# A hybrid decoder step on one core: a mask moved ahead of two key steps, and eight value pages requested later

## The reference, cut to what matters

```
z   = (q . k) / sqrt(64) + bias                    # stick-breaking attention, 8 heads
w_s = exp(log_sigmoid(z_s) + sum_{j>s} log_sigmoid(-z_j))
ya  = sum_s w_s v_s
yb  = rmsnorm(GLA(q, k, v, decay)) * silu(r)        # gated linear attention
h  += (sigmoid(g_a) * (ya @ U_a) + sigmoid(g_b) * (yb @ U_b)) @ W_o
h  += sum over 8 x 16 chosen experts of gate * gelu(h_n . u_e) * v_e
h  += (p @ W_ple) * sigmoid(rmsnorm(h) @ W_gate)
```

## Time and profile before

| | |
|---|---|
| median of 3 runs | 2042.43 us (2038.75 to 2044.11) |
| profiled execution | 2044.63 us, span 2043.0 us |
| TensorE, matmuls | 1544.6 us busy (76%) |
| VectorE | 1364.6 us busy (67%) |
| GpSimd | 776.2 us busy (38%) |
| ScalarE | 663.1 us busy (32%) |
| mean DMA rate | 378 GB/s over the span |

### The profile page before, as it was taken

How to read it: one execution, slowest core, us unless ns; L and a number is a source line. 1 busy time by engine, 2 the same in 40 slices (tenths; PEclk the granted TensorE clock), 3 DMA queues, 4 the chain that set the end, 5 groups by cost and what they waited for, 6 DMA issues and landing times. The chain is left out here.

```text
span 2043.0 us, 24165 instructions
## 1 busy us (share of the span) xinstructions
PE 1544.6 (76%) x8202; PEld 733.4 (36%) x8202; DVE 1364.6 (67%) x2607; ACT 663.1 (32%) x1850; POOL 776.2 (38%) x882
## 2 busy tenths in 40 slices
PE   8999889989987777776796677676457558476656
PEld 6647534665464333433321233332012112122112
DVE  3996999872187876556645467877577787545554
ACT  3222246401123444343323223332233423323224
POOL 2432333323624433333343443434343444444441
PEclk9999879999998998888898989998677778779778
DMA  7878989988989999999999999999999999999995
GB/s 247 276 269 316 355 298 334 352 327 308 367 326 398 419 419 416 419 415 418 411 417 421 394 420 418 417 399 420 416 390 402 394 399 422 388 413 420 421 421 230
DMA packets 158204, 771.88 MB, mean 378 GB/s; under 512 B 26928, under 2 KB 27496, under 8 KB 90496
## 3 DMA queue, kind: packets, MB, share of 16 engines
q0 software_dynamic: 103072, 637.59, 77.7%
q1 hardware_dynamic: 55008, 132.74, 17.8%
HBM read 762.03 MB, written 5.58 MB: 376 GB/s over the span
## 5 line engine op out<-in xcount | busy, mean ns | idle before, releaser
L2424 PE MATMUL bank<-arena 64*64 64x512 f32 x4096 | 635.4, 751 | 430.7 <-ACT arena L1288 426.0
L1801 DVE CUSTOM_DVE_ANT_0 arena<-arena 128x1024 f32<-128x1024 f32 x520 | 630.2, 1226 | 461.8 <-DMA arena<-experts_in,arena 457.9
L831 POOL DMA_INDIRECT arena<-experts_in,arena x520 | 585.1, 1125 | 859.3 <-PE bank L2424 738.5
L2424 PEld LDWEIGHTS bank<-arena 64*64 64x64 f32 x4096 | 158.4, 158 | 853.7 <-ACT arena L1288 623.1
L1277 ACT ACTIVATE arena<-arena 128x2 f32<-128x2 f32 x260 | 52.8, 203 | 881.1 <-DVE arena L1801 876.5
L778 POOL DMA_DIRECT2D arena<-cache_k_in x256 | 137.8, 538 | 303.4 <-DVE arena L1378 260.6
L1288 ACT ACTIVATE arena<-arena 128x64 f32<-128x64 f32 (+1 forms) x520 | 152.3, 340 | 8.5
L1373 DVE TENSOR_TENSOR arena<-arena 128x2048 f32<-128x2048 f32 x64 | 146.2, 2284 | 10.1 <-DMA arena<-cache_k_in 7.2
L1378 DVE TENSOR_REDUCE arena<-arena 128x32 f32<-128x2048 f32 x64 | 146.1, 2283 | 1.3
L204 DVE TENSOR_TENSOR arena<-arena 128x512 f32<-128x512 f32 (+9 forms) x215 | 130.0, 610 | 14.2 <-DMA arena<-xT_in 8.4
L2268 PE MATMUL bank<-arena 128*128 128x256 f32 (+1 forms) x512 | 126.4, 404 | 16.3 <-DMA arena<-w_stream_in 9.2
(11 more groups left out here) (128 smaller groups left out, 1368.8 us busy)
## 6 DMA issues: line engine op xcount, KB each, us to landing
arena<-cache_k_in POOLq DMA_DIRECT2D x256, 256.0 KB, 5.0
arena<-w_stream_in SPq DMA_DIRECT2D x125, 512.0 KB, 7.8
arena<-cache_v_in SPq DMA_DIRECT2D x160, 256.0 KB, 6.1
arena<-cache_v_in POOLq DMA_DIRECT2D x96, 256.0 KB, 6.0
arena<-experts_in,arena POOLq DMA_INDIRECT x520, 12.7
arena<-xT_in SPq DMA_DIRECT2D x4, 520.0 KB, 6.2
arena<-scratch_q SPq DMA_DIRECT2D x1, 2048.0 KB
arena<-x_rows_in SPq DMA_DIRECT2D x2, 1024.0 KB
```

The lines of the kernel that those rows point to most:

```text
L831: pool.indirect_dma_start(gring[:, s, :], None, A["experts"], bass.IndirectOffsetOnAxis(ap=rows, axis=0)).then_inc(g_landed[s], 16)
L1801: last = V.tensor_tensor_reduce(gring[:, s, 0:D], gring[:, s, 0:D], x_rows, 1.0, 0.0, ALU.mult, ALU.add, dot[:, s:s + 1])
L2424: last = mm(bank[2 * r + c2][out, :], diag[rows, s], gring[rows, s, cols], start=start, stop=True, skip_group_check=True)
```

## The change

Two edits. On VectorE, `own_heads(1)`, which followed two key steps after `ob_norm(3)`, now stands ahead of these two, so that 5 key steps follow it in place of 3. On SyncE, sample 4's halves 0 and 1 are asked for behind `g2` and `sk` in iteration 0 of the gates' loop, and its halves 2 to 7 in the iteration after the one in which they were asked for, each behind that iteration's weight tiles.

```diff
@@ sync
             sp.dma_start(h1A, A["x_rows"][0:2 * P].rearrange("(t p) c -> p t c", p=P)).then_inc(rows_landed, 16)
-            for n in range(14, 4 * PAGES // HALF_V + 2):
+            for n in range(14, 4 * PAGES // HALF_V):
                 early_half(n)
...
                     sp.dma_start(sk, A["sub_keysT"]).then_inc(second_landed, 16)
-                for b, half in V_IN_GATES.get(m, ()):
+                    early_half(4 * PAGES // HALF_V)
+                    early_half(4 * PAGES // HALF_V + 1)
+                for b, half in V_IN_GATES.get(m - 1, ()):
                     if half + 2 < V_ROUNDS * RING_V // HALF_V:
                         early_half(b * PAGES // HALF_V + half + 2)
@@ vector
                 ob_norm(h)
                 if h == 2:
                     scores_argument(1)
-                keys(2)
+                if h < 3:
+                    keys(2)
                 if h == 0:
                     scores_softplus(1)
             own_heads(1)
-            keys(3)
+            keys(5)
```

## The result

The changed kernel takes 2082.61 us (median of 6 runs, 2080.81 to 2086.52), the kernel before 2042.86 us in its 6 runs. The ratio is 1.0198, 95% interval 1.0184 to 1.0211: 40 us slower. The prediction said 2066 us, 2054 to 2080. The direction was right; the time lies above the range, because two terms were sized at half of what they cost. The title names eight pages, those of halves 0 and 1; the 24 pages of halves 2 to 7 also move, by one iteration, and they cost the most.

What follows compares the result with a forecast made beforehand. It took expert fetches, which neither edit touches, to fill most of the span, so only their start moves. 0 + 5.4 + 13.6 + 5.0 = 24.0 us on the median of 2042.43 gave 2066 us, range 2054 to 2080.

Steps and rivals of the forecast that it cites:

- The mask: VectorE's own_heads(1) ahead of two key steps: head_sums(0) still waits for VectorE's sums; priced at 0, bounds -1.5 to +3 us.
- Pages past the first weights: Sample 4's halves 0 and 1 ahead of gate 2's first tile on SyncE's queue: 5.4 us, bounds 4 and 6.5.
- 2.10 MB at the 362 GB/s of that stretch: The eight pages ahead of gate 2's first tile, moved at the DMA rate of 397 to 412 us: 5.8 us.
- The tile's own issue slips by about 1 us: Gate 2's first tile on SyncE, behind eight page issues of 4.14 us in all, is issued about 1 us later.
- Pages one gate later: Gates 3 to 6 each have one half asked for at the moment of use; net 2.1, 4.3, 5.0, 2.2: 13.6 us.
- the last page of a half is issued about 2.0 us after the up tile ends: SyncE in gates 3 to 6: the tile's own issue 0.4 us, then three more at 0.52 us each.
- 0.2 for the last matmuls: TensorE in gates 3 to 6: 0.2 us added after the last page's flight, before the next gate tile.
- The flights of 4.0 to 5.2 us: Time for a half's last page to land: 5.2, 4.0, 4.3 and 4.1 us in gates 3 to 6.
- The clock: TensorE in gates 5, 6 and 7, newly behind stops, at the low clock: 3 x 1.7 = 5.0 us, bounds 0 and 8.
- gate groups behind the stops take near 8.9 us: Sign expected in the profile after: TensorE's 32-matmul gate groups following a stop run near 8.9 us, against 7.18 us normally.
- Nothing behind the gates takes it up: From 495 to 600 us TensorE has no slack, so the gates' loss arrives at the first expert fetch and the end.
- the waits are long: Rival for the gates: flights of about 8 us and low clock through each following gate; 43 us, 2086 us, chance 0.09.

## Why the prediction was wrong, point by point

- **The mask, 0 us: right**, with its reason. VectorE's list sets the start of head_sums(0), and the experiment with the mask alone gives 0.9997.
- **Pages past the first weights, 5.4 us: the mechanism right, the size wrong.** The term "2.10 MB at the 362 GB/s of that stretch" gave the moved bytes the whole DMA. SyncE's queue had 211 GB/s of it while GpSimd's was filled, which makes 10.0 us; measured +11.9 in the changed kernel and +10.3 with this part alone. "The tile's own issue slips by about 1 us" was wrong too: it slips by 4.7 us, and the prediction didn't count the 1.9 us for page numbers. This is the step that failed here: the rate of one queue and the issue in front of the tile.
- **Pages one gate later, 13.6 us: the mechanism right, the size wrong**; measured 28.1. The step that failed is the sum of each gate's stretch: "the last page of a half is issued about 2.0 us after the up tile ends", plus its flight, plus "0.2 for the last matmuls". The largest miss is the 0.2: it was 1.8 us in each gate, 6.4 us in all, of which somewhat more than half is there at the high clock too, since the two matmuls of a page that comes alone take 1.03 us. The issue came 3.9 us behind the up tile in gates 3 and 4, because the page numbers are read between tile and pages: 4.3 us in all. The flights of 4.0 to 5.2 us were about right in gates 3 and 4 (5.6 and 4.1) and too short in gates 5 and 6 (5.5 and 6.3): 3.8 us in all.
- **The clock, 5.0 us: in the wrong place.** The engine did fall to the low clock in the page stops, but it paid in the pages' own matmuls (about 0.7 us behind each last page) and was back at the high clock early in the tiles: they take 0.3 us more in gates 5 and 6, and with gate 4's tile, which no longer follows a stop for weights, the sum is -0.6 us. The sign "gate groups behind the stops take near 8.9 us" didn't come.
- **Nothing behind the gates takes it up: right**, 39.2 of 41.4 us arrive at the first expert fetch.
- **The rivals.** The result lies nearest to "the waits are long" (43 us, chance 0.09), but by another route: flights of about 8 us and the low clock through each following gate were its cause, and the longest flight of a last page was 6.3 us. The range was too narrow because both its sides were made by the flight and the clock; the issue, the last matmuls and the queue's share stood in it at one value.

What stays open: where 2 of the 9 us of the run with half (4,3) later come from, since profiled executions differ by several us behind the gates anyway; why the flights of gates 5 and 6 were longer, and longer still with the numbers read ahead, beyond the nearness of GpSimd's burst; and how much of the +1.9 us at the start of gate 0 is chance.

## What to carry to other kernels

A request on a queue that also streams weights is not placed by "one stage later" but by the last wait in front of it: behind the third tile it cost 26 us, behind the first 4.5, and one half moved later with a whole stage still ahead of its use gained 9. When bytes are put ahead of a tile on one queue, divide them by what that queue gets beside the others, not by the DMA's rate, and count the address reads and issues in front of it. Count the last matmuls as they run behind a page that comes alone, not as they run in a row. For transfers that nothing waits for soon (g2 and sk), look for a place where both queues have gaps: in iteration 7, with half (4,3) later, the gates had no stop over 0.3 us, in iteration 5 the stop only moved. A gain of the whole time from iteration 7 over half (4,3) later alone isn't shown.

## What the runs showed of the hardware that was not expected

- Two filled queues share a full DMA nearly evenly by bytes, whichever asked first: 3.59 and 3.11 MB in 17 us (408 to 425 of the changed kernel), 1.49 and 1.42 MB in 430 to 438 us of the kernel before. The flights were 16.4 us for SyncE's pages, which had g2, sk and tiles issued just ahead of them, and 9.5 us for GpSimd's of the same size that were issued in the same 7 us.
- Reading eight page numbers holds SyncE for some 1.7 to 1.9 us: the first page that needs new numbers is issued 2.2 us behind the tile's issue in gates 3 and 4 (451.18 and 473.43), and 0.5 us behind it in gates 5 and 6; with the numbers read ahead it is 0.5 us in gate 3 too.
- The two matmuls of a value page that comes alone take 1.03 us at a granted clock of 1.00 and 1.88 us at 0.50 (changed kernel, 518.65), while the eight of four landed pages take 1.05 us together.
- With the same requests up to gate 2's first tile, the stop there was 3.71 to 6.15 us in six executions, and the group of 32 matmuls behind it 8.86, 9.59 or 10.19 us; the longest group followed a stop of 4.54 us and not the longest one.
- A page of 64 KB flew 1.9 us (median, gate 4), one of 256 KB 3.3 us in the same gate of the changed kernel.
- The start of the gates differs by up to 4.7 us between executions whose lists up to there differ little or not at all (384.93 with the halves a gate later, 389.63 in the mask's run, 389.54 with g2 and sk and half (4,3) later). In 294 to 297 us, in the heads, the granted clock is 0.82 in the first and 0.50 in the other two, so TensorE leaves the low clock there at different moments; but kernels that start the gates at 386.5 to 386.8 have 0.50 to 0.63 in the same window, so it isn't shown to be the whole cause.
